# Prompt attention with scores in four column groups of 32 keys and exponentials turned by VectorE

## The reference, cut to what matters

```python
CHUNK, SEQ, H_B, D_NOPE, D_ROPE, DV_B = 64, 2048, 8, 64, 32, 64
def block(args):                 # 128 queries
    qb, pb = args
    s = jnp.einsum('bqhd,bkhd->bhqk', qb, k) * scale
    mask = k_chunk[None, :] <= (pb // CHUNK)[:, None]
    p = jax.nn.softmax(jnp.where(mask[None, None], s, -jnp.inf), axis=-1)
    return jnp.einsum('bhqk,bkhd->bqhd', p, v)
# later: o_b * silu(z_b), beside the other branch, into the output projection
```

## Time and profile before

| | us |
|---|---|
| three runs | 3904.22, 3906.15, 3907.92 |
| median | 3906.15 |
| span of the profiled execution | 3905.3 |
| PE busy over the span | 3687.1 (94%) |
| DVE busy | 1749.4 (45%) |
| ACT busy | 1326.2 (34%) |
| POOL busy | 165.4 (4%) |

### The profile page before, as it was taken

The page is one execution under the profiler, slowest core; times in us unless marked ns, Lnnn a source line. Parts: engine busy times, 40 slices in busy tenths (PEclk is TensorE's granted clock), DMA queues, the critical chain, the costliest instruction groups (busy, mean ns, idle before and its releaser), DMA issues. The chain is left out here.

```text
span 3905.3 us, 62624 instructions
## 1 busy us (share of the span) xinstructions
PE 3687.1 (94%) x24668; PEld 2632.8 (67%) x24668; DVE 1749.4 (45%) x4469; ACT 1326.2 (34%) x3423; POOL 165.4 (4%) x191
## 2 busy tenths in 40 slices
PE   6999999969999888999999998999999999799998
PEld 3777777758888544666666445677767767677775
DVE  2443434446665234655555222221221122499996
ACT  1111111136665225655555001222122111355553
POOL 0000000011110000000000000000000000000100
PEclk8999999979999899999999999999999999899999
DMA  7111111132210011000001664111111111433433
GB/s 288 46 53 60 45 45 45 44 103 85 86 49 31 22 50 33 28 17 17 17 11 54 224 215 159 70 61 57 72 62 59 70 70 64 180 114 145 156 129 116
DMA packets 114815, 317.49 MB, mean 81 GB/s; under 512 B 30040, under 2 KB 48392, under 8 KB 109384
## 3 DMA queue, kind: packets, MB, share of 16 engines
q1 hardware_dynamic: 111864, 288.48, 20.1%
q0 software_dynamic: 2768, 26.47, 2.3%
HBM read 205.16 MB, written 109.74 MB: 81 GB/s over the span
## 5 line engine op out<-in xcount | busy, mean ns | idle before, releaser
L2352 PE MATMUL e_p<-e_hT,w_ahead 128*128 128x128 f32 x3264 | 411.4, 276 | 3.2 <-DMA shared<-w_in_o 3.2
L2352 PEld LDWEIGHTS e_p<-e_hT,w_ahead 128*128 128x128 f32 x3264 | 390.0, 193 | 11.3 <-issue 11.3
L535 PEld LDWEIGHTS a_p<-a_hT,w_even 128*128 128x128 f32 x3264 | 369.7, 193 | 9.4 <-issue 7.7
L535 PE MATMUL a_p<-a_hT,w_even 128*128 128x128 f32 x3264 | 369.9, 276 | 1.3 <-DVE a_hT L318 1.3
L550 PE MATMUL a_p<-w_even,a_hT 128*128 128x512 f32 (+2 forms) x1024 | 370.4, 522 | 0.0
L550 PEld LDWEIGHTS a_p<-w_even,a_hT 128*128 128x128 f32 x1024 | 194.0, 191 | 164.9 <-issue 115.8
L1675 DVE TENSOR_REDUCE q_mx<-q_sps 128x1 f32<-128x512 f32 (+4 forms) x320 | 181.4, 583 | 215.2 <-PE q_sps L1516 214.4
L2744 PE MATMUL h_b<-h_w,h_oT 128*128 128x512 f32 x512 | 236.6, 596 | 0.0
L2199 PE MATMUL c_b<-shared,c_oc 128*128 128x512 f32 x512 | 224.6, 598 | 9.2 <-DMA c_oc<-scr_ob 9.2
L2303 ACT ACTIVATE e_r<-e_p 128x512 f32<-128x512 f32 x66 | 39.4, 597 | 518.5 <-PE e_p L2358 298.7
L1604 ACT ACTIVATE q_P<-q_sps,q_mx 128x512 f32<-128x512 f32 (+4 forms) x320 | 190.6, 602 | 19.6 <-DVE q_mx L1680 14.9
(11 more groups left out here) (458 smaller groups left out, 6047.0 us busy)
## 6 DMA issues: line engine op xcount, KB each, us to landing
scr_qkg<-e_r SPq DMA_DIRECT2D x68, 512.0 KB, 2.6
h_rq<-scr_qkg SPq DMA_DIRECT2D x17, 2048.0 KB, 10.7
scr_iz<-e_r SPq DMA_DIRECT2D x34, 512.0 KB, 2.6
scr_qkv<-a_cv SPq DMA_DIRECT2D x17, 768.0 KB, 3.2
d_sc<-scr_qkv SPq DMA_DIRECT2D x17, 768.0 KB, 4.3
wa<-w_ada SPq DMA_DIRECT2D x8, 1536.0 KB, 16.2
w_ahead<-w_ada POOLq DMA_DIRECT2D x8, 1536.0 KB, 7.7
w_ahead<-w_in_o POOLq DMA_DIRECT2D x6, 2048.0 KB, 8.9
```

Of the source, the lines that this page charges most:

```text
L535: mm = pe.matmul(bank[g][:, (c % 4) * P:(c % 4 + 1) * P], w[:, k, c * P:(c + 1) * P], hT[:, p, k, :], start=k == 0, stop=k == KD - 1)
L2352: mm = pe.matmul(bank[n % 4][:, c * P:(c + 1) * P], w[k][:, a:a + P], hT[:, p, k, :], start=k == 0, stop=k == KD - 1)
```

## The change

The scores of a head are computed for 32 queries at a time. For each of the four query blocks u there are four matmuls i: weights are the 32 queries, the streamed operand is every fourth group of 32 keys (keys 32i to 32i+31 of each key tile), and the output lands on rows 32i to 32i+31. So the rows hold 4 key groups by 32 queries, the columns hold the key tiles. Now a 32x32 transpose of each block brings keys onto the rows, and DVE does that directly from on-chip memory to on-chip memory; PE's transposes and the copies of ACT and DVE are gone. The maximum of a query now lies spread over the four row groups: DVE reduces each, POOL copies three groups next to the first (`gathered`), DVE takes the lowest of the negated maxima, POOL copies the result to the three other groups (`top_r`). The sums are folded over the row groups by a small matmul once per tile (`sums`). The mask becomes a 97th contraction row: 1 for the first 64 queries, times 0 or -1e30 in kT; POOL writes that row in `keys` and opens it tile by tile. Up to g = 8 a head has one part of four query blocks, above that two parts of two; three score slots of 1024 columns are used in turn. All work that used spare columns of the score bank or the transpose banks now shares one bank `aux`, in two halves one after the other.

```diff
@@ keys, POOL
+            for half in kT:
+                hidden = half[HQ:HQ + 1, :, :].rearrange("p h (t c) -> p h t c", c=P)
+                pool.memset(hidden[:, :, :, 0:CH], 0.0)
+                pool.memset(hidden[:, :, :, CH:P], UNSEEN)
@@ attention, class Size
+                self.n = B * self.kt
+                self.own = 4 if self.kt <= 8 else 2
+                self.parts = PARTS // self.own
@@ attention, POOL
+            for z, h in heads_in_order:
+                n, p = no(z, h), no(z, h) % 2
...
+                pool.wait_ge(part_r, n + 1)
+                for i in range(1, 4):
+                    u = pool.tensor_copy(low[0:B, p, i, :], low[i * B:(i + 1) * B, p, 0, :])
+                u.then_inc(gathered, 1)
+                pool.wait_ge(low_r, n + 1)
+                for i in range(1, 4):
+                    u = pool.tensor_copy(top[i * B:(i + 1) * B, p, :], top[0:B, p, :])
+                u.then_inc(top_r, 1)
@@ attention, PE
+                for part in range(z.parts):
+                    since(pe, exp_r, z.slot(h, part) - SLOTS + 1)
+                    to = z.scores_of(h, part)
+                    for u in range(z.own):
+                        at = (part * z.own + u) * B
+                        for i in range(4):
+                            mm = pe.matmul(to[i * B:(i + 1) * B, u, :].rearrange("p (t c) -> p t c", c=B), qT[0:HQ + 1, z.m % 2, h, at:at + B],
+                                           keys[:, :, i * B:(i + 1) * B], start=True, stop=True)
+                    mm.then_inc(sc_r, 1)
+            def products(z, j):
+                pe.wait_ge(pt_r, no(z, 2 * j) + 2)
...
+                if a:
+                    scores(*a)
...
+                if b:
+                    scores(*b)
+                products(z, j)
@@ attention, ACT
+            def exps(z, h):
+                n = no(z, h)
+                act.wait_ge(top_r, n + 1)
...
+                        a = act.activation(Pr[:, n % 2, at, 0:z.n], of[:, u, :], ACT.Exp, bias=top[:, n % 2, at:at + 1],
+                                           accum_out=ls[:, z.m % 2, at, h:h + 1])
+                    a.then_inc(exp_r, 1)
@@ attention, DVE
+                nz = ahead(z, h, 1)
+                if nz:
+                    maxima(*nz)
+                if before:
+                    before()
+                turned(z, h, 0)
+                if nz:
+                    lowest(*nz)
+                for part in range(1, z.parts):
+                    turned(z, h, part)
```

More of the change, by code:

```diff
@@ L1457, in _ @@
             store(len(tiles) - 1)
-            for p in range(min(2, len(tiles))):
+            for p in range(2):
                 sp.wait_ge(stored[p], (len(tiles) + 1 - p) // 2 * 16)
@@ new lines, in queries, with queries_T @@
+            def queries(m, half):
+                pe.wait_ge(cqt_out, m + 1)
+                if half:
+                    since(pe, inv, m - 1)
+                else:
+                    pe.wait_ge(qb_out, 2 * m + 1)
+                for k in range(3):
+                    mm = pe.matmul(aux[:, 0:384], cqT[:, k, :], wu[:, k, half * 384:(half + 1) * 384], start=k == 0, stop=k == 2)
+                mm.then_inc(qps, 1)
+            def queries_T(m, half):
+                pe.wait_ge(roped, m + 1)
+                if half:
+                    pe.wait_ge(qT_out, 2 * m + 1)
+                elif m >= 2:
+                    pe.wait_ge(obT_r, m - 1)
+                for h in range(4 * half, 4 * half + 4):
+                    mm = pe.transpose(aux[0:HQ, h % 4 * P:(h % 4 + 1) * P], qb[:, h, :], ident[:, :])
@@ L1501, in scores @@
                 if h == 0:
[L1502 to L1543, removed]
+                    since(pe, seen, z.m)
+                    pe.wait_ge(ones, 1)
+                keys = kT[h // 4][0:HQ + 1, h % 4, :].rearrange("p (t c) -> p t c", c=P)[:, 0:z.kt, :]
@@ L1544, in products @@
+            def products(z, j):
+                pe.wait_ge(pt_r, no(z, 2 * j) + 2)
+                since(pe, oU_r, z.m * PAIRS + j)
+                for c in range(z.kt):
                     for p in range(2):
[L1545 to L1548, removed]
+                        mm = pe.matmul(ops[p * DV:(p + 1) * DV, 0:P], V[:, c, 2 * j + p, :], PT[:, (2 * j + p) % 4, c, :], start=c == 0, stop=c == z.kt - 1)
+                mm.then_inc(pv_r, 1)
@@ L1556, in pair @@
+                if j == 0 and z.m:
+                    sums(z.m - 1)
                 if j == 1 and after(z):
-                    queries(z.m + 1)
+                    queries(z.m + 1, 0)
                 if j == 2 and after(z):
[L1559 to L1566, removed]
-                    if b == z.mid and nz:
-                        scores(nz, 2 * nj + 1)
@@ L1576, in _ @@
+            for h in range(2):
+                scores(sizes[0], h)
             for z in sizes:
@@ L1611, in exps, with queries @@
-            def exps(z, h):
-                for b in range(z.nb):
-                    exp(z, h, b)
-            def turn(z, j, b):
-                act.wait_ge(tr_a, z.turned(j, b))
-                w = min(4, z.kt - 4 * b) * P
-                act.copy(PT[:, z.turned(j, b) % 2, 0, 0:w], tps[0][:, 0:w]).then_inc(pt_a, 1)
+                act.copy(cqT[:, :, :], aux[:, 0:384].rearrange("p (k t) -> p k t", k=3)).then_inc(cqt_out, 1)
+            def queries(m, half):
+                act.wait_ge(qps, 2 * m + 2 - half)
+                if half:
+                    since(act, qbt, 2 * m)
+                act.mul(qb[:, 4 * half:4 * half + 4, :], aux[:, 0:384].rearrange("p (h c) -> p h c", h=4), scale).then_inc(qb_out, 1)
@@ new lines, in maxima, with lowest @@
+                since(dve, top_r, n - 1)
+                for part in range(z.parts):
+                    dve.wait_ge(sc_r, z.slot(h, part) + 1)
+                    u = dve.tensor_reduce(low[:, n % 2, 0, part * z.own:(part + 1) * z.own], z.scores_of(h, part), AX, ALU.max, negate=True)
+                u.then_inc(part_r, 1)
+            def lowest(z, h):
+                n = no(z, h)
+                dve.wait_ge(gathered, n + 1)
+                if n >= 2:
+                    before, g = heads_in_order[n - 2]
+                    dve.wait_ge(exp_r, before.exps(g))
+                dve.tensor_reduce(top[0:B, n % 2, :], low[0:B, n % 2, :, :].rearrange("p i u -> p u i"), AX, ALU.min).then_inc(low_r, 1)
@@ new lines, in turned @@
+            def turned(z, h, part):
+                n = no(z, h)
+                if part == 0:
+                    since(dve, pv_r, n // 2 - 1)
+                to = PT[:, n % 4, 0:z.kt, :].rearrange("p t (u q) -> p u t q", q=B)
+                dve.wait_ge(exp_r, z.slot(h, part) + 1)
+                own = slice(part * z.own, (part + 1) * z.own)
+                u = dve.transpose(to[:, own], Pr[:, n % 2, own, 0:z.n].rearrange("p u (t k) -> p u t k", k=B))
+                if part == z.parts - 1:
+                    u.then_inc(pt_r, 1)
@@ L1722, in _ @@
             maxima(sizes[0], 0)
-            maxima(sizes[0], 1)
+            lowest(sizes[0], 0)
+            following(sizes[0], 0)
             for z in sizes:
```

270 lines of the change are left out of this document (120 added, 150 removed).

## The result

The changed kernel takes 3949.86 us (median of 4 runs, 3949.51 to 3950.88), the kernel before 3905.18 (4 runs beside them, 3903.38 to 3907.92): a ratio of 1.0116, 95% interval 1.0105 to 1.0128. It is slower by 45 us, where I had forecast it faster by 45. The time lies in the attention stage alone: it starts at 1498.06 instead of 1496.75 and its last result copy ends at 2186.47 instead of 2141.75, so it lasts 688.4 us, not 645.0. The forecast was 597 for this stretch: of its 600, 2 us lie ahead of the first scores and 1 us behind the last result copy.

What follows compares the result with a forecast made beforehand. PE was taken to bound the attention stage. Loops of 198 and 367 us, 32 once per tile and 3 at the ends make 600 against 645, so 3861 us in all; range 3822 to 3966.

Steps and rivals of the forecast that it cites:

- g: The number of key tiles of a tile, 1 to 16; the forecast's costs per head are written with it.
- score rounds: Scores on PE: four column groups side by side, 0.027 us per key tile a round, eight rounds a head.
- DVE's transposes: 32x32 transposes on DVE, priced like an addition of 1024 columns, 1.22 us, so equal to the maxima.
- Rivals B and C: DVE's transposes cost twice the addition, 103 us more, chance 0.08; column groups run two abreast, 127 us more, chance 0.06.
- POOL's phase: Three POOL copies between DVE's lowest and ACT's exponentials, taken as three small writes of 0.14 us, 0.55 us with handovers.
- x: Time from the end of DVE's lowest through POOL's three copies to ACT: 0.55 us, range 0.3 to 0.8.
- Rival A: POOL's copies stall beside DVE's work, 0.39 us more each, loops 140 us longer, 4001 us; chance 0.12, half of it milder.
- Loop B: Tiles above 8 key tiles, per head pair through PE's order: 2.2 + 0.739 us per key tile, deciding from 11 on.
- A granted clock under 0.9: One of the prediction's listed signs of being wrong: PE granted less than 0.9 of 2.4 GHz.
- Rival D: PE's clock falls to 1.2 GHz because PE waits inside the loop: 218 us more, 4079 us, chance 0.06.
- Once per tile for g up to 8: Query matmuls, transposes and gate product in tiles 0 to 7: 1 us per tile, 0 to 3.9 possible.
- The 2 us of the start: Start of the attention stage: 2 us later because queries and transposes share one bank.

## Why the prediction was wrong

Forecast and measurement part by 91 us in the stage: 206 against 254.3 in tiles 0 to 7, 391 against 434.1 in tiles 8 to 15.

- *Removal of PE's transposes, score rounds, products, DVE's transposes, maxima, exponentials*: right. 16 score instructions of 480 columns take 1.80 us, four rounds of 0.027 x 15 = 0.405 and a start: four column groups run side by side, as the row had it for three. The lower factor of the Trainium skill (TensorE: Matmul & The Clock Gate, Measured speedup vs the span model) does not hold here. Transposes of 1024 columns take 1.233 us, summed as 1.24. Rivals B and C are out.
- *POOL's phase*: mis-sized. Three copies take 0.62 us instead of 0.42, so x is 0.71, not 0.55; 64 heads make at most 10 us of it in tiles 0 to 7 (a turn at g = 8 is 0.11 us longer than forecast, which would be 7). Rival A showed in two places, once per tile: POOL's gather beside the gate product, which reads two on-chip operands (1.04 us instead of 0.62, 15 times), and its spread beside the rotation, which does too (0.76 to 1.39 us, 9 times; the first two rows are from tile 0); beside transposes and maxima POOL kept its pace.

```profile
1513.69 0.41 DVE L1667 TENSOR_TENSOR q_rt<-q_qb,q_cs 128x256 f32<-128x256 f32 x1
1513.82 0.76 POOL L1479 COPY q_top<-q_top 32x4 f32<-32x4 f32 x3 [0.26 <-DVE q_top L1687]
...
2076.55 0.20 DVE L1715 RECIPROCAL q_rc<-q_aux 128x8 f32<-128x8 f32 x1
...
2076.70 1.04 POOL L1475 COPY q_low<-q_low 32x4 f32<-32x4 f32 x3 [6.07 <-DVE q_low L1678]
2076.78 0.69 DVE L1719 TENSOR_TENSOR q_G<-q_zb,q_rc 128x512 f32<-128x512 f32 x1
```

- *Loop B, the first step that failed*: its terms were right to some 5 us, its clock was not. I summed a wait of PE for ACT into every pair and kept all PE terms at 2.4 GHz, since PE at 93% had run at 0.98. That row has PE's mean share, not its longest wait. A granted clock under 0.9 stood among the prediction's own signs of being wrong, and it came: 0.88 here. Rival D saw the clock, but as all or nothing (218 us, 0.06); it came in pieces, behind single waits, at 38 us. The Trainium skill (TensorE: Matmul & The Clock Gate, HAM oscillation — how this bites in real kernels) describes that pattern for a loop that waits for a DMA: the wait sends PE into each turn cold; it advises to restructure the loop so that PE stays warm. This trace shows the pattern, with ACT in the place of the DMA, by 2.85 us of waiting and 8.48 us at 0.60, and the changed order agrees with the advice (tiles 8 to 15 at 1.00).
- *Once per tile for g up to 8, the second step that failed*: 1 us taken, with 3.9 as the upper end. (254.3 - 198 - 10) / 8 = 5.8 was measured, on the mean. I looked for what lies beside ACT; but PE's work for the next tile stands in one queue with the scores and goes through one bank, so each piece waits for a copy of ACT or a product of DVE that stands behind a head's loop. The wait at the fold alone is 3.28 us in tile 7; moving it gave 14 us, and moving the gate product and the rotation gave 33 more once the orders were changed.

In sum 38 for the clock in tiles 8 to 15, 10 for x and 38 for the work once per tile in tiles 0 to 7, 5 of rest, which the longer x could make up in tiles 8 to 15 (40 phases of 0.16 by the forecast's loops): 91. How much of the 38 is the wait and how much the half clock behind it was not separated; where the gate product and the rotation moved, 20 of 33 us were the wait. The 2 us of the start did not come: from the stage's first transposes to the first scores it takes 12.35 us, where it took 12.17.

## What to carry to other kernels

When a change takes work off the bound engine and puts a loop over three others in its place, look at that engine's longest single wait, not at its mean share: behind waits of 2.5 to 3.6 us TensorE here mostly worked on for 3 to 7 us at half speed. Work that isn't due yet, such as the products of the pair before, belongs into that wait; and an order is changed on all engines that meet at its semaphores: on DVE alone it made this kernel 51 us slower. Here the operations of the change were worth 76 us in the best order that was tried, and its first order lost 120 against that one.

## What the hardware showed that was not expected

- Copies of 32x4 cost 0.19 us each on POOL and 0.16 on DVE, so six of them per head made DVE 123 us busier over the 128 heads.
- Added matmuls made a kernel 36 us faster (waits filled in tiles 8 to 15), and in another place 12 us slower at a higher granted clock (0.99 instead of 0.88 in tiles 0 to 3).
